# A seven-slot weight ring and five places for the heads, instead of eight and four

## The reference

```python
x = x + g1 * token_mixer(modulate(rms_norm(x, ...), sh1, sc1), ...)
u = causal_depthwise_conv(h @ w_up, ffn_dw_w, ffn_dw_b)
a, b = split(u, 2);  x = x + g2 * ((silu(a) * b) @ w_down)
```

## Time and profile before

| | us |
|---|---|
| median of 3 runs | 2625.11 |
| lowest and highest run | 2624.48, 2625.7 |
| the profiled execution, its own time | 2623.43 |
| its span in the trace | 2621.6 |

### The profile page before, as it was taken

The page is one execution under the profiler, slowest core; times in us unless marked ns, Lnnn a source line. Parts: engine busy times, 40 slices in busy tenths (PEclk is TensorE's granted clock), DMA queues, the critical chain, the costliest instruction groups (busy, mean ns, idle before and its releaser), DMA issues.

```text
span 2621.6 us, 38515 instructions
## 1 busy us (share of the span) xinstructions
PE 2581.4 (98%) x15546; PEld 2229.8 (85%) x15546; DVE 1747.9 (67%) x2815; ACT 1086.5 (41%) x1685; POOL 67.9 (3%) x59
## 2 busy tenths in 40 slices
PE   8999999999999999999999999999999999999998
PEld 4789889877898899978888888888898888887997
DVE  5678777656787777757674458665677765387554
ACT  3546366535453675422223334222333222356442
POOL 0000000000000000100001010000000000100000
PEclk9999999999999999999999999999999999999999
DMA  8663467655634676464452213544435544231553
GB/s 329 229 194 111 148 208 248 220 196 196 198 108 172 221 244 217 151 215 178 161 193 91 98 62 137 185 153 145 145 122 193 187 170 163 82 121 65 179 184 113
DMA packets 120880, 441.13 MB, mean 168 GB/s; under 512 B 13312, under 2 KB 14720, under 8 KB 120192
## 3 DMA queue, kind: packets, MB, share of 16 engines
q1 hardware_dynamic: 120704, 438.68, 48.9%
HBM read 437.58 MB, written 1.05 MB: 167 GB/s over the span
## 4 chain that ended last, share of the span: by engine, by line
PE 93%; DVE 3%; ACT 2%; DMA 1%; issue 0%; SPq 0%; DVEq 0%; ACTq 0%
PE ps L657 24%; PE ps L658 24%; PE ps L659 24%; PE ps L661 14%; PE ps L654 5%; PE ps L655 3%; DMA ring<-stream 1%; DVE rests L1918 1%; PE ps L669 1%; ACT heads L1379 0%; DVE rs L1978 0%; DVE h_split L2034 0%; DVE rt L2025 0%; DVE rs L2018 0%; DVE rt L2182 0%
## 5 line engine op out<-in xcount | busy, mean ns | idle before, releaser
L657 PE MATMUL ps<-h_split,heads 128*128 128x256 f32 (+1 forms) x3192 | 1028.8, 322 | 7.1 <-DVE rests L1918 3.5
L658 PE MATMUL ps<-h_split,heads 128*128 128x256 f32 (+1 forms) x3192 | 1014.9, 318 | 0.0
L659 PE MATMUL ps<-h_split,rests 128*128 128x256 f32 (+1 forms) x3192 | 1014.6, 318 | 0.0
L1918 DVE TENSOR_TENSOR rests<-ring,heads 128x1024 fp32r<-128x1024 f32 x548 | 665.7, 1231 | 189.9 <-ACT heads L1379 182.9
L1379 ACT ACTIVATE heads<-ring 128x1024 fp32r<-128x1024 f32 x548 | 568.2, 1056 | 471.9 <-DMA ring<-stream 218.6
L657 PEld LDWEIGHTS ps<-h_split,heads 128*128 128x128 f32 x3192 | 610.0, 191 | 81.4 <-ACT rt L1558 15.1
L658 PEld LDWEIGHTS ps<-h_split,heads 128*128 128x128 f32 x3192 | 610.4, 191 | 42.3 <-issue 1.9
L659 PEld LDWEIGHTS ps<-h_split,rests 128*128 128x128 f32 x3192 | 610.1, 191 | 40.2
L1945 DVE SCALAR_TENSOR_TENSOR qt<-ring,silu_rows 128x1024 f32<-128x1024 f32 x240 | 286.5, 1231 | 5.2 <-issue 1.8
L657 PE MATMUL ps<-hid_split,heads 128*128 128x512 f32 (+1 forms) x660 | 236.3, 358 | 0.0
L659 PE MATMUL ps<-hid_split,rests 128*128 128x512 f32 (+1 forms) x660 | 235.7, 357 | 0.0
(11 more groups left out here) (229 smaller groups left out, 2425.2 us busy)
## 6 DMA issues: line engine op xcount, KB each, us to landing
ring<-stream SPq DMA_DIRECT2D x822, 512.0 KB, 3.5
consts<-constants SPq DMA_DIRECT2D x1, 1728.0 KB, 10.9
x_sb<-x_in SPq DMA_DIRECT2D x1, 1024.0 KB, 11.4
x_sb<-ctx_in SPq DMA_DIRECT2D x1, 1024.0 KB, 4.8
silu_rows<-rows_in SPq DMA_DIRECT2D x1, 1024.0 KB, 7.7
out<-area SPq DMA_DIRECT2D x1, 1024.0 KB, 4.8
consts<-constants SPq DMA_DIRECT2D x1, 704.0 KB, 9.3
cols<-columns SPq DMA_DIRECT2D x1, 538.5 KB, 10.1
```

Of the source, the lines that this page charges most:

```text
L657: nc.tensor.matmul(out, lhsT[0], rhs[0], start=first, stop=False)
L658: nc.tensor.matmul(out, lhsT[0], rhs[1], start=False, stop=False)
L659: ins = nc.tensor.matmul(out, lhsT[1], rhs[0], start=False, stop=last)
L1918: nc.vector.tensor_tensor(rests[:, u % RING, :], ring[:, u % RING, :], as_f32(heads[:, n % HEADS_RING, :]), ALU.subtract)\
```

## The change

Two constants change: the ring gets seven slots instead of eight, and the heads get five places instead of four. A slot and a place are both 4 KB on each partition, so the memory used is the same.

```diff
--- before.py
+++ after.py
@@ -43,8 +43,8 @@
 EPS = 1e-6
 FIRST_SPLITS = (0, 1, 3, 5)
 UB = 8
-RING = 8
-HEADS_RING = 4
+RING = 7
+HEADS_RING = 5
 PAIR_UNITS = 2 * KD // UB
 BANKS = 6
 ROWS_BANK, COLS_BANK = 6, 7
```

## The result

| | before | after |
|---|---|---|
| median, us | 2625.4 | 2712.46 |
| lowest and highest run | 2624.48, 2627.4 | 2710.05, 2717.46 |
| span of the profiled execution | 2621.6 | 2712.5 |
| mean granted clock of TensorE | 0.995 | 0.979 |
| PE busy | 2581.4 | 2621.2 |

The change makes the kernel slower: 1.0336 times, interval 1.0323 to 1.035, or 87 us. The sign was forecast. The size was not: the forecast said 27, its range ended at 42.

What follows compares the result with a forecast made beforehand. PE, 93% of the chain, was taken as the bound, so only its waits counted. Terms 11.8 + 7.1 + 2.4 + 4.4 + 1.0 + 1.4 - 1.4 gave +26.7 us, forecast as a median of 2652 us, range 2636 to 2667.

Steps and rivals of the forecast that it cites:

- The start of up_0 and up_1: H129 directly behind H126 waits for its landing, so unit 130 starts 5.9 us late; two layers +11.8 us (8.0 to 15.4).
- The mixer starts: H40 lands 2.9 us later and R42 stands ahead of L2281, delaying PE's row sums; both layers +7.1 us.
- The first softmax: R82, 1.2 us, now stands ahead of L2121, and PE's transpose waits for that softmax; two layers +2.4 us.
- The norm: Behind the first layer, R208 moves ahead of L1978 and PE waits for L1988 behind it; +1.0 us, once.
- what is won: Waits before L654 in the second layer's downward products (1.2 us) and 0.2 us of L1918 waits go; -1.4 us.
- The merged branches: H110 and R110 are put ahead of L2383, with 0.1 us of room; two layers +4.4 us (2.4 if the copy finds a gap).
- The gates of the convolution: H57's landing moves back with L1624 behind it, which PE waits for; 0.7 us twice, +1.4 us (0 to 2.6).
- That cover fails only where landings are late, which is what the terms above are: Steady stretches (attention, downward products) cost nothing: ACT waits for a place there and units landed long before.
- The worse rival: Landings of 7.0 us in both up stages, nothing won, one further pair per stage hit by 3.7 us: 2667 us, chance 0.13.
- Every term at its idle time alone: PE's matmuls keep their order and number, so only PE's waits were counted, +26.7 us in all.
- What would have shown it wrong: No such PE idle time in up_0, early-requested landings at 3.3 us throughout, or new idle time mainly in the second block.

Runs made afterwards that it cites:

- The slot alone: Kernel before with seven ring slots instead of eight, four places and its order kept: 2651.17 us, ratio 1.0104.
- the order alone: Changed kernel's order and five places with eight slots, three rotation tables and the mask left out for room: 2665.44 us, ratio 1.016.
- The two experiments on this: Kernel before with extra head copies at units 129 and 318, 2638.29 us; changed kernel with throwaway products ahead of ten PE waits, 2691.41 us.
- the order alone without the rows' waits: Eight slots, five places, the changed kernel's order, tables and mask left out, ACT's copy of guests' rows ahead of the pair's splits: 2642.47 us, ratio 1.0062.
- The filled kernel: Changed kernel with 39 throwaway products on PE, 1 to 6 ahead of each of ten long waits: 2691.41 us, ratio 1.0247.

## Why the prediction was right in sign and wrong in size

- **The start of up_0 and up_1** (11.8, of it 5.9 in up_0): right, to a tenth of a microsecond in when H129 and unit 130 start. The reading of unit u's landing from that of unit u+1 held. The new idle time is 4.1 us there and 4.3 in up_1, less than the 5.9: in up_0 the matmuls of unit 129 had become 1.7 us slower and filled a part of it. The slot alone made 2.8 us of new idle time at each start, the order alone 2.6 and 2.8.
- **The mixer starts** (7.1): 6.2 us of idle time, 4.3 of them at the row sums that the step names. L2281 stands behind R41 and R42 as forecast (DVE and PEld of after, against the earlier trace rows):

```profile
87.91 2.36 DVE L1918 TENSOR_TENSOR rests<-ring,heads 128x1024 fp32r<-128x1024 f32 x2 [4.03 <-ACT heads L1379]
...
90.98 0.22 PEld L661 LDWEIGHTS ps<-sq,consts 64*32 64x32 f32 x8 [2.69 <-DVE qt L2281]
```

- **The first softmax** (2.4): 4.9. The step priced the moved R82, which cost what it said, 1.2 us and 0.2 of wait for its copy. It left out H79, ahead of it on ACT, which waited for its landing already before: unit 79 is now issued when unit 80 was, and lands 6.0 us after its issue instead of 5.1. PE was 9.6 us late up to there, H79 is 10.9, so DVE comes to the softmax 1.2 us later for it. With R82 behind that, less the 0.27 of room, PE waits 2.3 us more in the first layer (H79 of before; then of after H79, R82 and PE's row):

```profile
185.33 1.06 ACT L1379 ACTIVATE heads<-ring 128x1024 fp32r<-128x1024 f32 x1 [4.55 <-DMA ring<-stream]
...
196.19 1.06 ACT L1379 ACTIVATE heads<-ring 128x1024 fp32r<-128x1024 f32 x1 [5.80 <-DMA ring<-stream]
...
206.48 1.23 DVE L1918 TENSOR_TENSOR rests<-ring,heads 128x1024 fp32r<-128x1024 f32 x1 [0.21 <-ACT heads L1379]
...
209.36 0.52 PE L669 MATMUL ps<-consts,work 128*128 128x128 f32 x3 [2.92 <-DVE work L2132]
```

- **The norm** (1.0) and **what is won** (1.4): right. The norm's new idle time is 0.8, and at the second layer's downward products the waits of 0.49 and 0.68 us at the L654 named are gone. **The merged branches** (4.4): 3.0 of idle time, between the 4.4 and the 2.4 that the step gave for a copy that finds a gap. That the table has 4.3 for it is luck: 1.3 of them are slower matmuls, which the step did not count.
- **The gates of the convolution** (1.4): 2.7, above the step's bound of 2.6. The step asked who stands behind the late copy on ACT, found L1624, and priced it here. It did not ask where else L1624 stands behind a split.
- **"That cover fails only where landings are late, which is what the terms above are"**: this step failed. With it the list of places was closed, and the pairs of the up stages behind the first were left at nothing. Counting nothing held for the downward products, for the attention behind its first softmax and for nearly the whole second block, where from 1200 us of before's time to its end only 1.7 us are added. It failed for the pairs of the up stages that end a guest's rows: seven waits with 26.2 us of new idle time, and 20.3 us of slower matmuls behind them. The cover named, ACT waiting for a place, was not there in these stages even before: from 380 to 484 us, in up_0, ACT waited 3.3 us ahead of L1379 for landings and never for a place. Copies that moved forward met their landings there, in the pair of the rows or a few pairs ahead, and L1624 stood behind them.
- **The worse rival and its refusal.** It had the mechanism, a further pair hit behind the next plain units, but one of a stage and by the price of a slow transfer. It was turned down because PE's delay would give "ACT and the ring those 6 us as room". That is wrong: SP issues a unit when PE has used the one seven earlier, so a late PE makes the transfers late with it, and the distance between issue and need stays what the ring allows. Unit 141 was issued at 411.4, 23.9 us later than unit 142 before, and PE was 24.0 us late by then.
- **Every term at its idle time alone**: the second step that failed. The argument took "PE working off matmuls, whose order and number the change leaves alone" as fixed work. 39.8 us were added to them at a lower clock, 18.0 of it at the places named, which is why 28.1 forecast there became 44.0. The two experiments on this show the idle time as the cause for ten waits and two waits; for the mixer starts and the softmax it is argued from the same rows.
- **What would have shown it wrong**: none of the three signs came. PE had new idle time in up_0, the units asked for early landed after 5.2 us (129) and 6.4 us (141) and not after 3.3, and only 4.9 of the 51.1 us lie in the second block. Two of the signs watched terms that the forecast named and the third the second block: none could show the later pairs of the up stages, which had no term.

By the medians the 87 us come apart as: the slot alone 26, the order alone without the rows' waits 17, the rows' waits behind splits that land late 45, in sum 88. In each of these the slower clock is included; by the pairing it is 40 of the 91.

What stays open: of the 13.1 us of slower matmuls outside the ten filled waits, 3.3 lie in the stretch at 2436 with no wait ahead of it, and for the other 10 the idle time as the cause is argued, not shown. The filled kernel won 21 us by the medians, where 24.9 us of slower matmuls went; the rest may be idle time that the filler left (up to 1.05 us at a place) or the filler's own overrun. The second layer's softmax (2.6 us) was not taken apart.

## What to carry to other kernels

When a step is moved forward on an in-order engine and can wait, list every instruction of other work that now stands behind it, in each loop iteration and not only where the move was noticed; an unrelated copy of 0.58 us was worth half of this loss. A lookahead that is filled at a stage's start sets the distance for the whole stage, so its depth must fit what the transfers deliver: the ring's slots, not the places for results. On TensorE price a wait as its idle time and the slower matmuls behind it, read from rows of the same kernel that follow a wait. And let one sign of being wrong watch the whole span, such as the idle time outside the places named.

## What the runs showed of the hardware

- Behind a wait of 3.83 us TensorE lost 1.5 us to the lower granted clock, behind one of 9.52 us 2.1 us; in the changed kernel the seven waits for the rows, of 1.9 to 5.5 us and 26.2 in all, lost 20.3 us behind them. Here several short waits cost more than one long one.
- TensorE's granted clock also fell with no idle time: to 0.50 at 2436 us of the changed kernel, behind 32 products of one column each that followed one another; the same place in before ran at 1.00.
- A product of 512 float32 columns took 0.87 us, in two instructions, while the 256-column matmuls of the rounded parts follow one another at 0.12 us (unit 130 of before: 24 of them, 2.76 us from the first start to the last).
- Transfers of 512 KB that were issued within 0.4 us of each other landed after 5.5 and 6.4 us; in the same 25 us of this stage the fastest took 3.2.
